# A two-block transformer kernel on one Trainium2 core: hand-overs between matrix stages rearranged, the opening load halved, the last rows shared with GpSimd

## The reference

```python
# first block (one layer, an mLSTM mixer)
h = h + 0.5 * rmsnorm(swiglu(rmsnorm(h, gn[0]), ffn_w_in[i, 0], ffn_w_out[i, 0]), gn[1])
u = rmsnorm(h, gn[2])
y = mlstm_mixer(u, a_w_in[j], a_conv_w[j], a_conv_b[j], a_gate_b[j], a_w_out[j])
h = h + rmsnorm(y, gn[3])
h = h + 0.5 * rmsnorm(swiglu(rmsnorm(h, gn[4]), ffn_w_in[i, 1], ffn_w_out[i, 1]), gn[5])
return h[:, N_META:]
# second block (two layers)
h = h + gated_deltanet(rmsnorm_2(h, ...), ...)                 # layer 0
h = h + conv_gated_mlp(rmsnorm_2(h, ffn_norm_w[0]), ...)
k_sh, v_sh = shared_kv(h, kv_norm_w, w_kv)                     # layer 1
h = h + sliding_window_sink_attention(rmsnorm_2(h, ...), k_sh, v_sh, ...)
h = h + conv_gated_mlp(rmsnorm_2(h, ffn_norm_w[1]), ...)
return rmsnorm_2(h, final_norm_w)
```

## Time and profile before

| what | us |
|---|---|
| median of the runs (lowest, highest) | 1353.02 (1345.2, 1355.68) |
| profiled execution, its own time | 1350.6 |
| its span in the profile | 1348.8 |
| TensorE busy | 1277.2 (95%) |
| VectorE busy | 980.0 (73%) |
| ScalarE busy | 765.5 (57%) |
| GpSimd busy | 253.8 (19%) |

### The profile page before, as it was taken

How to read it: one execution, slowest core, us unless ns; L and a number is a source line. 1 busy time by engine, 2 the same in 40 slices (tenths; PEclk the granted TensorE clock), 3 DMA queues, 4 the chain that set the end, 5 groups by cost and what they waited for, 6 DMA issues and landing times.

```text
span 1348.8 us, 28806 instructions
## 1 busy us (share of the span) xinstructions
PE 1277.2 (95%) x10587; PEld 1244.5 (92%) x10587; DVE 980.0 (73%) x1665; ACT 765.5 (57%) x1269; POOL 253.8 (19%) x233
## 2 busy tenths in 40 slices
PE   6999999999999999999968999999989998999997
PEld 6999999988999999988867999999989988999997
DVE  5766557876867755797799554789976786799954
ACT  5544445696554444579834554566665565666652
POOL 0000000010000000044406102345540021355500
PEclk9999999999999999999988999999999999999998
DMA  7555564563366656464527113865556523565563
GB/s 234 179 174 169 141 175 140 175 193 95 112 202 186 178 159 192 139 212 136 170 82 211 35 48 117 205 197 182 178 157 194 189 79 110 157 185 177 159 184 105
DMA packets 76733, 212.87 MB, mean 158 GB/s; under 512 B 7973, under 2 KB 22389, under 8 KB 76528
## 3 DMA queue, kind: packets, MB, share of 16 engines
q1 hardware_dynamic: 73536, 202.47, 49.3%
q0 software_dynamic: 2832, 9.04, 3.0%
q10 hardware_dynamic: 288, 0.33, 0.1%
HBM read 208.74 MB, written 3.06 MB: 157 GB/s over the span
## 4 chain that ended last, share of the span: by engine, by line
PE 61%; DVE 20%; issue 8%; DMA 4%; ACT 4%; POOL 2%; DVEq 1%; SPq 0%; ACTq 0%
PE bank L501 14%; PE bank L503 14%; PE bank L502 13%; DVE wl L394 4%; DVE cv L802 3%; DMA raw<-in_w_up 2%; DVE tp L782 2%; DVE cv L799 1%; PE bank L1549 1%; DVE sc L799 1%; DVE dVT L2219 1%; PE bank L2673 1%; PE bank L2763 1%; PE bank L1551 1%; DVE gTmp L2285 1%
## 5 line engine op out<-in xcount | busy, mean ns | idle before, releaser
L389 ACT ACTIVATE wh<-raw 128x1024 fp32r<-128x1024 f32 (+3 forms) x428 | 409.4, 963 | 312.3 <-PE bank L503 234.3
L394 DVE TENSOR_TENSOR wl<-raw,wh 128x1024 fp32r<-128x1024 f32 (+3 forms) x385 | 426.5, 1116 | 148.7 <-ACT wh L389 147.8
L501 PE MATMUL bank<-XH,wh 128*128 128x256 f32 (+1 forms) x1456 | 415.5, 285 | 13.5 <-DVE XL L890 7.0
L503 PE MATMUL bank<-XH,wl 128*128 128x256 f32 (+1 forms) x1456 | 413.0, 284 | 0.0
L502 PE MATMUL bank<-XL,wh 128*128 128x256 f32 (+1 forms) x1456 | 412.8, 284 | 0.0
L501 PEld LDWEIGHTS bank<-XH,wh 128*128 128x128 f32 x1456 | 275.6, 189 | 16.1 <-DVE XL L890 7.7
L503 PEld LDWEIGHTS bank<-XH,wl 128*128 128x128 f32 x1456 | 276.0, 190 | 0.0
L502 PEld LDWEIGHTS bank<-XL,wh 128*128 128x128 f32 x1456 | 274.7, 189 | 0.0
L501 PE MATMUL bank<-AH,wh 128*128 128x256 f32 (+1 forms) x704 | 199.0, 283 | 6.4 <-DVE wl L394 4.1
L394 POOL TENSOR_TENSOR wl<-raw,wh 128x1024 fp32r<-128x1024 f32 x43 | 113.3, 2637 | 480.0 <-ACT wh L389 479.8
L503 PE MATMUL bank<-AH,wl 128*128 128x256 f32 (+1 forms) x704 | 198.5, 282 | 0.0
(11 more groups left out here) (375 smaller groups left out, 2268.9 us busy)
## 6 DMA issues: line engine op xcount, KB each, us to landing
raw<-in_w_up SPq DMA_DIRECT2D x176, 512.0 KB, 4.3
raw<-in_w_down SPq DMA_DIRECT2D x64, 384.0 KB, 3.5
raw<-in_w_down SPq DMA_DIRECT2D x64, 320.0 KB, 3.1
raw<-in_w_gvz SPq DMA_DIRECT2D x32, 512.0 KB, 4.4
raw<-in_w_gqk SPq DMA_DIRECT2D x16, 512.0 KB, 5.1
raw<-in_w_gout SPq DMA_DIRECT2D x16, 512.0 KB, 4.5
raw<-in_w_mv SPq DMA_DIRECT2D x8, 512.0 KB, 5.0
raw<-in_w_mqk SPq DMA_DIRECT2D x8, 512.0 KB, 5.0
```

Of the source, the lines that this page charges most:

```text
L389: eng.activation(WH[s][:, 0:n, :], raw[s][:, 0:n, :], ACT.Copy).then_inc(s_hi[s], 1)
L394: eng.tensor_tensor(WL[s][:, 0:n, :], raw[s][:, 0:n, :], WH[s][:, 0:n, :].bitcast(F32), ALU.subtract).then_inc(s_lo[s], 1)
L501: eng.matmul(out, WH[s][:, i, :], xh, start=start, stop=False)
L503: mm = eng.matmul(out, WL[s][:, i, :], xh, start=False, stop=stop)
```

## The change

It makes these edits:

- `Root.spread` uses transposes in place of float32 products with the identity, in all eleven norms.
- `walk`: in the last unit of a `NormedSteps` stage ACT's square stands ahead of the split of the next stage's fourth unit.
- `AddSteps.dve`: where several groups end in one unit, the addition of the next group stands ahead of the low part and square sum of this one.
- `warm(Sqrt)` stands behind the steps of mout0, gout0 and so0 instead of ahead of them.
- `keep_warm` behind the three spreads: 3 in place of 6.
- Opening: chunk 0 of `H` and the k=0 half of slot 0's weights (every second tile) come first, then chunk 1 and the other half; slot 0 is split in halves; `s_lo` is set ahead of all waits on DVE and POOL; the larger part of `vec` (541 columns) is issued by POOL behind the last piece of `H` in place of ACT, and waited for ahead of the squares.
- End: DVE finishes 6 chunks. ACT multiplies chunks 6 and 7 by the gain into `YG` ahead of the root, TensorE spreads the column a second time into bank 6, ACT copies it to `R`, POOL multiplies the two chunks by it, and SP stores them from `YG`.

```diff
+                            if last and u == U - 1 and kind == "act" and isinstance(c, NormedSteps):
+                                c.act(eng, it, u)
                             if n < U:
                                 split(eng, kind, st, it, n)
...
+                        elif last and u == U - 1 and kind == "act" and isinstance(c, NormedSteps):
+                            pass
...
-                    mm = eng.matmul(self.b[:, t:t + P], RC[:, i:i + 1].to_broadcast([P, P]), ident, start=True, stop=True)
+                    mm = eng.transpose(self.b[:, t:t + P], RC[:, i:i + 1].to_broadcast([P, P]), ident)
...
+                groups = [g for g in range(self.G) if self.st.unit_of[g] == u]
+                for n, g in enumerate(groups):
+                    if n == 0:
+                        self.add(eng, it, g)
+                    if n + 1 < len(groups):
+                        self.add(eng, it, groups[n + 1])
+                    self.rest(eng, it, g)
...
+            if kind == "act":
+                n1.high(eng, 0)
+                eng.wait_ge(s_first, 16)
+                eng.activation(WH[0][:, 0:TILES:2, :], raw[0][:, 0:TILES:2, :], ACT.Copy).then_inc(s_first_hi, 1)
+                n1.high(eng, 1)
+                eng.wait_ge(s_raw[0], 16)
+                eng.activation(WH[0][:, 1:TILES:2, :], raw[0][:, 1:TILES:2, :], ACT.Copy).then_inc(s_hi[0], 1)
...
+            if kind in ("act", "dve"):
+                eng.wait_ge(s_in2, 16)
             for c in range(DC):
                 if kind == "act":
                     n1.square(eng, c)
...
             if kind == "act":
-                warm(eng, ACT.Sqrt)
                 c_so0.act(eng, 0, 3)
                 c_so0.dv.wait(eng, 0, "acc3")
+                warm(eng, ACT.Sqrt)
             go(so1, c_so1)
...
             if kind == "act":
+                for c in (DC - 2, DC - 1):
+                    evacuated(eng, down4, down4.iters - 1, 1)
+                    eng.activation(YG[:, c, 0:SEQ], H[:, c, META:TM], ACT.Identity, bias=0.0,
+                                   scale=gains["gfin"][:, c:c + 1]).then_inc(s_tail, 1)
                 n10.root(eng)
+                eng.wait_ge(s_sp2, 1)
+                eng.activation(R[:, 0:SEQ], bank[6][:, 0:SEQ], ACT.Copy).then_inc(s_r2, 1)
...
-                for c in range(DC):
+                for c in range(DC - 2):
...
+            if kind == "pool":
+                eng.wait_ge(s_r2, 1)
+                for c in (DC - 2, DC - 1):
+                    eng.wait_ge(s_tail, c + 3 - DC)
+                    eng.tensor_tensor(YG[:, c, 0:SEQ], YG[:, c, 0:SEQ], R[:, 0:SEQ], ALU.mult).then_inc(s_fin2, 1)
...
+            eng.dma_start(H[:, 0:1, :], a["h0"][:, 0:1, :]).then_inc(s_h0[DC // 2], 16)
+            w0 = up1.weights[0].rearrange("p (g k) m -> p g k m", g=4)
+            eng.dma_start(raw[0][:, 0:TILES:2, :], w0[:, :, 0, :]).then_inc(s_first, 16)
+            eng.dma_start(H[:, 1:2, :], a["h0"][:, 1:2, :]).then_inc(s_h0[0], 16)
+            eng.dma_start(raw[0][:, 1:TILES:2, :], w0[:, :, 1, :]).then_inc(s_raw[0], 16)
...
+            eng.dma_start(vec[:, VEC["acw"]:VECS], a["vecs"][:, VEC["acw"]:VECS]).then_inc(s_in2, 16)
             eng.dma_start(cst[:, :], a["consts"]).then_inc(s_cst, 16)
...
-            eng.wait_ge(s_in, 32)
+            eng.wait_ge(s_in, 16)
...
             a1.spread(eng)
-            keep_warm(eng, 6)
+            keep_warm(eng, 3)
```

More of the change, by code:

```diff
@@ L468, in multiply_opening @@
             for u in range(SLOTS):
-                eng.wait_ge(s_lo[u], turn(st, 0, u) + 2)
+                if st is up1 and u == 0:
+                    eng.wait_ge(s_first_lo, 1)
+                else:
+                    eng.wait_ge(s_lo[u], turn(st, 0, u) + 2)
                 for j in (0, 1):
@@ L473, in multiply_opening @@
                     eng.wait_ge(s_xh, n.x0 + k + 1)
+                    if st is up1 and k == 1:
+                        eng.wait_ge(s_lo[u], turn(st, 0, u) + 2)
                     for g in range(G):
@@ new lines, in rest @@
+            def rest(self, eng, it, g):
+                m, T, h = it * self.G + g + self.m0, self.st.T, self.place(it, g)
+                for i, (gain, hi, lo) in enumerate(self.norms):
+                    self.ac.wait(eng, it, f"high{i}_{g}")
+                    self.dv.done(eng.scalar_tensor_tensor(lo[:, bass.ds(m, 1), 0:T], h, v(gain, m),
+                                                          hi[:, bass.ds(m, 1), 0:T].bitcast(F32), ALU.mult,
+                                                          ALU.subtract), f"low{i}_{g}")
+                self.ac.wait(eng, it, f"sq{g}")
+                self.dv.wait(eng, it, f"acc{(g - 1) % self.G}", back=int(g == 0))
+                self.dv.done(eng.tensor_tensor(ACC[:, 0:T], ACC[:, 0:T], SQB[g % 2][:, 0:T], ALU.add), f"acc{g}")
@@ L3578, in _ @@
             run_dma(eng)
-            for c in range(0, DC, 2):
+            for c in range(0, DC - 2, 2):
                 eng.wait_ge(s_fin, c + 2)
                 eng.dma_start(a["out"][:, c:c + 2, :], H[:, c:c + 2, META:TM]).then_inc(s_out, 16)
+            eng.wait_ge(s_fin2, 2)
+            eng.dma_start(a["out"][:, DC - 2:DC, :], YG[:, DC - 2:DC, 0:SEQ]).then_inc(s_out, 16)
             eng.wait_ge(s_out, 16 * DC // 2)
@@ L3674, in _ @@
             n10.spread(eng)
+            for i, t in enumerate((0, P)):
+                mm = eng.transpose(bank[6][:, t:t + P], RC[:, i:i + 1].to_broadcast([P, P]), ident)
+            mm.then_inc(s_sp2, 1)
 def _tiles(w):
```

64 lines of the change are left out of this document (32 added, 32 removed).

## The result

The changed kernel takes 1344.4 us (median of 22 runs, 1337.98 to 1350.81) against 1351.88 us of the kernel before in runs beside it (22 runs, 1342.14 to 1358.22). The ratio is 0.9951 [0.9935, 0.9966]: 7.5 us faster by the medians. The forecast was 1341.5 (1334 to 1351), with terms that sum to -10.3.

The account below looks back on a forecast made before the run. TensorE, busy 95% of the span, bounds the kernel, through its idle or half-clock stretches and its own work. Terms sum to -10.3: 1340.3 from the profiled 1350.6, 1342.7 from the median; middle 1341.5 us, range 1334 to 1351.

Parts of the forecast that it names:

- opening: Program start: earlier first product and squares near 16.7 bring up1's second iteration forward; -1.7 us (0 to -2.9).
- down1 to mv: Full norm after down1: earlier square, cheaper spread and fewer fill-ins start mv sooner; -1.3 us (-0.7 to -2.0).
- down2 to gz0: Full norm after down2: 0.5 from the order, 0.4 from the spread; -0.85 us (-0.4 to -1.5).
- mout1: Full norm after mout1: moved table load delays the split 0.5, spread returns 0.35; +0.1 us (-0.6 to +0.6).
- spreads in dense work: Six norms inside TensorE's dense work: fewer instructions, at 0.112 us each; -1.55 us (-0.8 to -1.6).
- gout: gout0 to gout1: interleaved groups end the fourth square sum 1.55 earlier; -1.5 us (-0.5 to -1.9).
- so: so0 to so1 to up4: moved table load and interleaved groups bring the last low part earlier; -2.7 us (-1.0 to -3.5).
- the end: After down4: DVE finishes six chunks instead of eight, so the last store issues earlier; -0.8 us (+0.5 to -1.3).
- rival C: Opening: `vec` lands late and the opening gives nothing, or part of the halves stalls; 1343.5 us, chance 0.16.
- the last wait for `XL` shorter by that: Sign in the profile after, at up4: TensorE's last wait shrinks as the split behind so0 comes 2.7 us earlier.
- Rival A: Hand-overs and norms: less activity brings more half-clock stretches, slower than before; 1346.5 to 1358 us, chance 0.07.
- Rivals B and D: First: gout and so give 1 together, 1345 us, chance 0.17. Second: half-clock stretch vanishes, opening gives 2.9; 1336.5, chance 0.22.

Follow-up runs that it names:

- x12: Changed kernel with x1, x2 and x3 joined, and the table load of down3 and down4 behind their last unit; 1335.07 us, ratio 0.9875.
- x1: Changed kernel with the wait for the larger part of `vec` behind the opening's squares and square sums; 1338.67 us, ratio 0.9907.
- x3: Changed kernel with the last low part of gout1's and so1's weights on DVE instead of GpSimd; 1341.08 us, ratio 0.9923.
- x6: Changed kernel with ACT's square behind the fourth slot's split again, at down1, mout1 and down2; 1350.49 us in one run.
- x4: Changed kernel with all spreads as float32 products with the identity again, instead of transposes; 1344.21 us in one run.
- x9: Changed kernel with ACT's table load ahead of the squares of mout0 and so0 again; 1341.58 us in one run.
- x5: Changed kernel with 6 instead of 3 fill-in products behind the three full spreads; 1334.09 us in one run.
- x14: x13 with 6 instead of 3 fill-in products behind the three full spreads; 1327.94 us, ratio 0.9811.
- x2: Changed kernel with ACT's table load behind the last unit of mout1, gout1 and so1; 1343.17 us, ratio 0.9937.
- x13: x12 with GpSimd's low parts in the first iterations of up3 and up4 given to DVE; 1330.17 us, ratio 0.9857.
- x7: Changed kernel with the whole opening as in the kernel before; 1341.80 us, ratio 0.9925.

## Why the prediction was right, and where it was not

The medians moved by -7.5, and the measured median, 1344.4, lies 2.9 above the forecast. The sum was -10.3, and the stretches of the profiles give about -8.5:

| term | forecast | measured | by |
|---|---|---|---|
| opening | -1.7 | -0.8 | 24.97 to 24.20 |
| down1 to mv | -1.3 | -0.9 | 22.86 to 21.93 in x12, both with one fall |
| down2 to gz0 | -0.85 | -0.7 | 19.33 to 18.67 |
| mout1 | +0.1 | -0.5 to +0.3 | 21.98 to 21.4 and 22.3, by where the fall lies |
| ahead of it, mout0 and mout1 | not in the sum | -0.7 | 29.45 to 28.75 |
| spreads in dense work | -1.55 | -1.6 | 0.34 at the first (0.83 to 0.49, the last end included) and 0.22 at one of two instructions less: 2 x 0.34 + 4 x 0.22 |
| gout | -1.5 | -1.4 | 28.09 to 26.71 |
| so | -2.7 | -1.7 | 21.70 to 19.97 |
| the end | -0.8 | -0.7 | 10.25 to 9.51 |

**Opening: the mechanism held, the size failed at one step.** ACT was free at 15.4 (forecast: near 16), but I put `vec` "at 16.7", and it came at 17.96. It was issued at 13.20, within the 12 to 13.5 of the forecast; the flight was 4.8 where I had carried over about 3.4, although I had written that up to 1 MB of loads lay ahead. Whether the loads in flight or GpSimd's queue made it longer, no run separates. For this term rival C came true, and the fall behind the wait took back the rest: the spread of down1, put "near 215", came at 216.92. x1 shows that the full slack was there: with the wait out of the way the second iteration is 3.6 earlier, more than my end of 2.9.

**so: a cost that I looked for in the wrong place.** I forecast the fourth sum near 1132.4, or 5.6 behind the start of so1 at 1126.82; it ended 7.3 behind it (1125.81 - 1118.54). The missing 1.7 is the held `XL`, as x3 shows. The row was there before the change: the first low part of the earlier trace rows's stretch took 0.81 where its neighbours took 0.48, with the table load ahead of it hiding the rest. I asked whether GpSimd holds up DVE only at the end, and answered it with operations that have one operand in PSUM. That answer holds there: the six last products take 0.472 to 0.479, beside GpSimd. It says nothing of `XL`, whose operands are both in SBUF. The Trainium skill, "SBUF — State Buffer", section "Who interferes with whom", has just this distinction: a DVE instruction with two SBUF inputs contends with a GpSimd instruction that reads SBUF, and the later one waits for the whole of the other. The trace agrees: 2.33 against 0.49 with GpSimd away, and the `H<-bank,H` additions stay at 0.41.

**The forecast "the last wait for `XL` shorter by that" was wrong as a sign to look for.** It is 3.33 in both kernels. All came 1.7 earlier, and what went was the first wait of up4, 1.90 before and 0.17 after. DVE's pace of 2.93 per group sets the later ones, as I had said of the chain itself.

**Full norms: right for down1 and down2, with two errors that cancel; at mout0 a term was missing.** From the last product to DVE's first step on `YG` it was 5.36 and is 3.64. x6 puts 0.99 on the order, where I had 0.65: I had let DVE's low part hold the inverse, but it ended within 0.15 of the root in both kernels (217.19 against 217.23 before, 216.78 against 216.64 now), so the whole 0.96 of the exchange came through. x4 puts 0.39 on the spread, where I had 0.7, because I took the half-clock duration of 1.27 as one end. The rest, 0.3, is the fall at 217.9 in the kernel before. For mout1 I had let the moved table load cost 0.5 and gain DVE 0.95 in a stretch that begins with its last product; it gained 0.6 ahead of that, since TensorE no longer waited for `YG` in mout1 (x9).

**The fill-ins: they count at half clock alone, and there the forecast was right.** At full clock three in place of six gave nothing (x5: 5.26 and 5.07, as with three). At half clock six hold TensorE: in the kernel before the first product of mv started 0.71 behind its `XH` and that of gz0 0.75, in x14 that of up2 0.75. With three it is 0.14 or 0.15 in every hand-over, ten with a fall among them. So of the 2.27 that the first product of mv came earlier, 1.72 are the chain's and 0.55 the fill-ins'; I had put 2.0 on both.

**Rival A, the clock, came in part.** The two profiled executions have the same clock, 0.981, and differ by 10.0 us. That is a lucky pair: among the 22 runs of the changed kernel none has a higher clock. Over all runs with a clock listed, before has 0.9798 +- 0.0008 (49 runs, mean 1351.9 us) and after 0.9774 +- 0.0012 (22 runs, 1344.1 us). Within each kernel, 0.001 of clock goes with 0.87 +- 0.18 us (least squares over all runs). So 0.0024 is some 2.1 us, and at equal clock the change is worth 10.0 +- 1.5 us, which is the sum that I had. Part of what was lost again may lie at 24.9, behind TensorE's wait in the opening: the 46 runs with that wait (after, x2, x3) have 0.9775 +- 0.0009, the 25 with x1's remedy (x1, x12, x13, x14) 0.9810 +- 0.0011. x7, with the opening as it was, has 0.9790 +- 0.0013. But these kernels differ in more than that wait, and x1 alone (0.9794 +- 0.0020) is not told from the changed kernel. One fall of 3.4 us is worth 0.0013 of the mean clock (half of 3.4 in 1338), so that in the opening can explain half of the 0.0024 at most. Whether fewer fill-ins or transposes, which the rival named, have a part in the rest is open. Against it: x13, with both, has 0.9820 +- 0.0020 over 6 runs, not below the kernel before, and six fill-ins added to it (x14) 0.9834 +- 0.0025 over 5. For it: x4 and x5, which take back one each, show 0.982 and 0.986, above all 22 runs of the changed kernel, but are one run each. The Trainium skill, "TensorE: Matmul & The Clock Gate", Part 4, on which that rival leaned, says that transposes don't count as busy for the gate in the same way; no run here shows an effect of it, nor excludes one.

**Rivals B and D.** gout and so gave 3.1 together, not 1, so B did not come; nor did D: the falls behind the waits of up4 are still there (6.8 us at 1137.7), and the opening did not give its 2.9.

**What stays open.** The stretches give about 8.5 and the equal-clock comparison 10.0 +- 1.5, which hardly differ. Up to 0.9 of it can lie in the falls: x6 and x4 together put 1.38 on down1 to mv and 1.10 on down2 to gz0, where the stretches with one fall in each kernel give 0.93 and 0.66; that is argued, not shown. Why the DeltaNet core, in which but one spread was changed, takes 258 to 269 us from one profile to the next was not looked into, and with it most of the 5.1 us that it gives to the 10.5 between the two spans are chance. x2, x3 and x7 were each not told apart from the changed kernel by their times; what they show rests on stretches.

## What to carry to other kernels

A wait that is moved to a queue behind other loads must be priced with those loads in flight, and should stand where its data is first read, not where the old wait stood. Before a step is moved, ask what it was hidden under: here a table load lay free beside a GpSimd instruction that held DVE, and moving it away cost 0.8 us, while the same move at a stage without that instruction gained 0.6. Compare two kernels over many runs by time and granted clock together; a single pair of profiles here showed 10.0 us where the medians showed 7.5.
